# Product-key expert layer: ranking, dense products and choosing spread differently beside the gathers

## The chip, the cores and the metric

The kernel is one program on one core of a Trainium2 chip. Its engines are TensorE (PE, matrix products), VectorE (DVE), ScalarE (ACT), GpSimd (POOL, which issues the gathers) and SyncE (SP, which issues plain DMAs). The metric is the device time of the program in microseconds: 2412.99 us before the change, the median of three runs (2411.26 to 2419.2).

## What is computed

Two blocks follow each other on 512 tokens of width 1024. The first 1106 us hold everything up to the queries of the last layer and are not touched by the change. The rest is `peer`, cut here to its core:

```python
q = (xb @ w_query).reshape(TOKEN_BLOCK, P_HEADS, 2, P_HALF)
s = einsum('thpk,hpnk->thpn', q, sub_keys)
sv, si = top_k(s, P_TOPK)                    # 16 of 128 keys, twice per head
cand = sv[:, :, 0, :, None] + sv[:, :, 1, None, :]
fv, fpos = top_k(cand, P_TOPK)               # 16 of the sums per head
eidx = take_along_axis(si0 * 128 + si1, fpos)    # ids of 128 experts per token
g = softmax(fv)
act = gelu(einsum('td,thkd->thk', xb, u_tab[eidx]))
return einsum('thk,thkd->td', g * act, v_tab[eidx])
```

There are four tiles of 128 tokens. Each token picks 128 of 16384 experts (8 heads by 16), and each expert is a row of 1024 floats in `u_tab` and one in `v_tab`, in HBM.

## The kernel before

**Two ways to the products with u.** For the token tiles 0 and 1 the u rows are gathered: POOL issues one indirect DMA per expert place k (128 rows, 512 KB) and DVE takes a dot product of each row with its token (`dot`, L1972). For the tiles 2 and 3 PE computes the products with all 16384 experts: 128 dense products, each of a block of 128 experts (512 KB, loaded by SP in plain DMAs into three buffers in turn) with 256 tokens, 8 matrix instructions (`dense`, L1082). A product waits for its block; ACT copies each pair of them out of PSUM (L2502). Of these results each token needs 128, and choosing them is the work called `ext`: in each of two rounds (over the results of products 0 to 63, then of 64 to 127, which take the same place in SBUF) there are 66 steps. In a step PE spreads ids (L1109), ACT makes a one-hot matrix of them (L2513, L2515), and PE two steps later multiplies it with the results (L1095). After every fourth step DVE compares, multiplies and sums (L2010, L2015, L2019). The second round's step 33 (step 99 in all) completes tile 2: DVE adds the rounds (L2024), ACT takes the Gelu, DVE makes the weights.

**The values.** For every tile the v rows are gathered, again 128 gathers of 512 KB, and PE sums them with their weights (L1145): in each of 32 m-steps four gathers, 16 matrix instructions (the trace shows 16 weight loads and 16 products per m-step). The weights stand in a window that ACT writes (L2547). A last step on DVE (`finish`, L2034 to L2044) adds and normalises a tile.

**The stages.** POOL's gathers run in the order of `STAGES`: U0, V0, U1, V1, V2, V3, each of 128 gathers. All share 17 slots of 4 KB per partition; a gather waits until the last user of its slot is done (a dot or a value product). A gather of a U stage waits for the ids of its half (`tk_e`, L1919), and in U1 also for the dense product that the table places 8 gathers before it.

**What sets the order.** The table `BESIDE` says what lies beside the gathers of a stage. An entry `(what, a, z, first, last)` spreads pieces a to z evenly over the positions first to last: k of 0 to 127 in a U stage, m of 0 to 31 in a V stage. All engines read it, each emits its own part of a piece at that position, and each works through its instructions strictly in order. `topk` are ranking parts: 60 of them for the tiles 2, 3 and 1, 20 for each tile (eight heads' rankings, L1844 to L1860, with pair steps and decoding; the ids come with L1919 or the line behind it, the weights with ACT's L2485 behind DVE's L1955). Part 49 completes the first half of tile 1's ids, part 59 the second. `ids` is a transpose of a tile's ids on PE (L1065), which waits for them. `dense` and `ext` are counted over all stages, 128 and 132 in all. Key products on PE (L1042) go with the ranking parts.

Of the kernel before, what the change touches and what calls it, by code (L numbers as in the profile page):

```python
# [37 lines left out]
for _n, _w in ROWS:  # L38
# [15 lines left out]


BESIDE = {
    ("U", 0): [("topk", 0, 22, 10, 124), ("ids", 0, 1, 12, 12), ("ids", 1, 2, 122, 122), ("dense", 0, 64, 0, 127)],
    ("V", 0): [("topk", 22, 40, 0, 14), ("topk", 40, 50, 15, 31), ("ids", 2, 3, 17, 17), ("ext", 0, 32, 1, 15),
               ("ext", 32, 66, 18, 31)],
    ("U", 1): [("topk", 50, 60, 0, 36), ("ids", 3, 4, 44, 44), ("dense", 64, 124, 0, 127)],  # L60
    ("V", 1): [("dense", 124, 128, 0, 2), ("ext", 66, 120, 3, 31)],
    ("V", 2): [("ext", 120, 132, 0, 6)],
    ("V", 3): [],
}

# [2806 lines left out]
```

## Time and profile before

| | |
|---|---|
| median of 3 runs | 2412.99 us |
| profiled execution | 2416.05 us |
| its span | 2414.2 us |
| PE busy | 2126.6 us, 88% |
| DVE busy | 1308.9 us, 54% |
| POOL busy | 885.7 us, 37% |
| ACT busy | 643.5 us, 27% |
| data moved by DMA | 590.01 MB, mean 244 GB/s |

Busy times overlap between engines. PE's matrix products are pipelined and their ends are modelled, so its busy time isn't work at full rate. A view by stretches has one line for a stretch: start and end, length, then for each engine the busy time and the number of instructions (with PEld the weight loads), then the granted TensorE clock as a share of full speed (1.00 is 2.4 GHz, 0.5 is 1.2 GHz), the busy share of the DMA engines and GB/s. Where the view is of one source line alone, only PE and PEld stand ahead of those. A share of DMA can come out slightly over 1. A line of a view in time has the start, the duration, engine, source line, operation, tiles, shapes and count, and in brackets the idle time of that engine just before it and what ended it. A stage is bounded here by the issue of its first gather and of the next stage's first: U0 begins at 1106 us, V0 at 1370, U1 at 1591, V1 at 1824.6, V2 at 2016.6, V3 at 2211. The work of PE and DVE on a stage lies some microseconds later.

### The profile page before, as it was taken

How to read it: one execution, taken by the hardware profiler on the slowest of the kernel's cores; microseconds unless marked ns; L12 is line 12 of the kernel's file. 1: busy time of each engine (PE TensorE's matmuls, PEld its weight loads, DVE VectorE, ACT ScalarE, POOL GpSimd, SP SyncE). 2: the span in 40 equal slices, each digit the busy share in tenths (PEclk: the TensorE clock that was granted, in tenths of full speed). 3: DMA queues.
4: the chain of work that ended last, by engine and by line, in shares of the span. 5: the costliest groups of instructions: out<-in, count | busy, mean ns of one | idle time of the engine just before them, and what ended most of it. 6: DMA issues, size and time to landing. Idle time of an engine off the chain costs nothing.

```text
span 2414.2 us, 31160 instructions
## 1 busy us (share of the span) xinstructions
PE 2126.6 (88%) x12429; PEld 1576.2 (65%) x12429; DVE 1308.9 (54%) x2914; ACT 643.5 (27%) x1077; POOL 885.7 (37%) x821
## 2 busy tenths in 40 slices
PE   6999889999999997899899988899898887875775
PEld 6786879889887875887788744567786454311111
DVE  3865476776456466556988775489763233100000
ACT  3335332322354333331111133421111343200000
POOL 0410000000000000002666655556766665666664
PEclk8999999999999998999999988889999898887898
DMA  4211245444212210225999998989999999999997
GB/s 178 70 36 46 112 154 198 181 174 157 89 69 105 70 53 18 88 70 185 366 415 417 406 346 312 336 309 412 413 411 419 378 343 327 348 378 368 356 374 284
DMA packets 147056, 590.01 MB, mean 244 GB/s; under 512 B 16336, under 2 KB 16464, under 8 KB 134240
## 3 DMA queue, kind: packets, MB, share of 16 engines
q0 software_dynamic: 110592, 402.70, 43.7%
q1 hardware_dynamic: 35136, 178.80, 19.7%
q10 hardware_dynamic: 1184, 6.53, 0.7%
q8 instruction: 98, 1.61, 0.3%
q14 instruction: 46, 0.38, 0.0%
HBM read 584.29 MB, written 3.67 MB: 244 GB/s over the span
## 4 chain that ended last, share of the span: by engine, by line
PE 33%; POOL 9%; DVE 8%; issue 8%; another core or an unknown queue 6%; DMA 4%; ACT 3%; SPq 0%; POOLq 0%; DVEq 0%; ACTq 0%
PE ps L1145 7%; PE ps L1082 6%; POOL big L2655 6%; PE ps L1095 5%; PE ps L556 4%; PE ps L557 4%; PE ps L558 4%; DVE cols L1972 2%; DMA big<-vtab,big 2%; DMA raw<-ucols 2%; POOL hres L2655 1%; ACT Ir L2513 1%; PE ps L1109 1%; ACT Ir L2515 1%
## 5 line engine op out<-in xcount | busy, mean ns | idle before, releaser
L1082 PE MATMUL ps<-rowb,raw 128*128 128x256 f32 x2048 | 464.4, 387 | 24.9 <-DMA raw<-ucols 22.1
L1082 PEld LDWEIGHTS ps<-rowb,raw 128*128 128x128 f32 x2048 | 391.6, 194 | 94.4 <-issue 20.8
L1145 PE MATMUL ps<-big,cols 128*32 128x512 f32 x1380 | 365.2, 692 | 77.6 <-issue 55.1
L2655 POOL DMA_INDIRECT big<-vtab,big x345 | 332.1, 963 | 190.9 <-issue 84.0
L2578 POOL TENSOR_TENSOR small<-small,cols 128x1 f32<-128x1 f32 (+3 forms) x33 | 28.9, 876 | 896.2 <-DVE small L1590 387.8
L1145 PEld LDWEIGHTS ps<-big,cols 128*32 128x32 f32 x1380 | 73.6, 121 | 254.0 <-issue 164.2
L2655 POOL DMA_INDIRECT big<-utab,cols x144 | 178.3, 1238 | 110.3 <-issue 36.6
L1972 DVE CUSTOM_DVE_ANT_0 cols<-big 128x1024 bf16<-128x1024 f32 x144 | 173.9, 1226 | 39.5 <-DMA big<-utab,cols 29.5
L1095 PE MATMUL ps<-Aj,Ir 128*128 128x64 f32 x1024 | 161.7, 301 | 27.3 <-issue 19.7
L2015 DVE TENSOR_TENSOR cols<-cols,ps 128x512 f32<-128x512 f32 x64 | 43.9, 688 | 253.0 <-remote 124.1
L2502 ACT ACTIVATE Aj<-ps 128x512 f32<-128x512 f32 x64 | 68.1, 1067 | 418.5 <-PE ps L1082 342.4
L556 PE MATMUL ps<-xhb,whb 128*128 128x512 f32 (+1 forms) x432 | 167.2, 387 | 5.9 <-ACT fbig L2356 3.0
L1095 PEld LDWEIGHTS ps<-Aj,Ir 128*128 128x128 f32 x1024 | 144.5, 214 | 38.1 <-issue 25.6
L557 PE MATMUL ps<-xhb,wlb 128*128 128x512 f32 (+1 forms) x432 | 164.1, 380 | 0.0
L558 PE MATMUL ps<-xlb,whb 128*128 128x512 f32 (+1 forms) x432 | 163.8, 379 | 0.0
L2034 DVE TENSOR_TENSOR cols<-ps,g2b 128x512 f32<-128x512 f32 x8 | 5.2, 688 | 271.3 <-remote 139.5
L2513 ACT ACTIVATE Ir<-ps,cols 128x512 f32<-128x512 f32 x128 | 87.7, 685 | 234.0 <-remote 123.8
L556 PE MATMUL ps<-whb,ah 128*128 128x256 f32 x512 | 146.0, 285 | 1.1 <-DVE al L1624 1.1
L1145 PE MATMUL ps<-hres,cols 128*32 128x512 f32 x408 | 137.1, 738 | 10.3 <-issue 5.7
L557 PE MATMUL ps<-whb,al 128*128 128x256 f32 x512 | 143.9, 281 | 0.0
L558 PE MATMUL ps<-wlb,ah 128*128 128x256 f32 x512 | 143.8, 281 | 0.0
L2109 ACT ACTIVATE whb<-raw 128x2048 fp32r<-128x2048 f32 x51 | 97.5, 1912 | 164.3 <-DMA raw<-ff 106.8
(388 smaller groups left out, 4479.7 us busy)
## 6 DMA issues: line engine op xcount, KB each, us to landing
raw<-ucols SPq DMA_DIRECT2D x128, 512.0 KB
raw<-ff SPq DMA_DIRECT2D x32, 1024.0 KB, 4.9
raw<-w SPq DMA_DIRECT2D x24, 1024.0 KB, 4.9
raw<-ada SPq DMA_DIRECT2D x24, 1024.0 KB, 4.8
raw<-wo SPq DMA_DIRECT2D x8, 1024.0 KB, 4.9
raw<-wq SPq DMA_DIRECT2D x8, 1024.0 KB, 4.8
big<-vtab,big POOLq DMA_INDIRECT x345
hres<-x SPq DMA_DIRECT2D x8, 512.0 KB, 6.4
```

The source lines that it names most:

```text
L556: e.matmul(o, lhsT=lh, rhs=rh, start=(k == 0), stop=False)
L557: e.matmul(o, lhsT=ll, rhs=rh, start=False, stop=False)
L558: ins = e.matmul(o, lhsT=lh, rhs=rl, start=False, stop=(k == n - 1))
L1082: ins = e.matmul(PS[b][:, c:c + 256], lhsT=un[j % NU][:, k, :], rhs=h2T[k // 4][:, k % 4, :], start=(k == 0), stop=(k == 7))
L1095: ins = e.matmul(PS[b][:, c:c + JC], lhsT=Ir[:, (g % 2) * 512 + q * 128:(g % 2) * 512 + (q + 1) * 128], rhs=Atd[:, 4 * g + q, :], start=Tr ...
L1145: ins = e.matmul(PS[hf][32 * j:32 * j + 32, :], lhsT=win[:, c0:c0 + 32], rhs=gs[i][:, hf * 512:(hf + 1) * 512], start=(m == 0), stop=(m == ...
L1972: e.tensor_tensor_reduce(out=junk[k % 3], in0=gs[i], in1=h2[:, t, :], scale=1.0, scalar=0.0, op0=ALU.mult, op1=ALU.add, accum_out=act[:, t ...
L2015: e.tensor_tensor(jm[n % 2], jm[n % 2], PS[(5, 7)[n % 2]][:, :], ALU.mult).then_inc(*V.mark("ex_p", (r, n)))
L2109: e.activation(hi, raw_of(n), ACT.Copy).then_inc(*A.mark("hi", u))
L2502: e.activation(Adt[:, jl:jl + 2, :], PS[2 + pair % 2][:, :].rearrange("p (j t) -> p j t", j=2), ACT.Copy).then_inc(*A.mark("dv", pair))
L2513: e.activation(one, PS[KEYS2[g % 2]][:, :], ACT.Abs, bias=pidx).then_inc(*A.mark("ex_a", r, g))
L2655: e.indirect_dma_start(gs[i], None, utab if st == "U" else vtab, bass.IndirectOffsetOnAxis(ap=idx, axis=0)).then_inc(sems[f"l_g{i}"], 16)
```

## The change

Only the table changes. In U0 26 ranking parts in place of 22. In V0 14 parts in 13 m-steps and then 10 in 8, in place of 18 in 15 and 10 in 17; and 50 choosing steps in place of 66. U1 takes the 16 choosing steps in its first 24 positions, and has 44 dense products, from position 24 on, in place of 60 from position 0 on. V1 begins with 20 dense products in 12 m-steps in place of 4 in 3, and has 34 choosing steps in the other 20 in place of 54 in 29. V2 has 32 choosing steps in 25 m-steps in place of 12 in 7.

```diff
 BESIDE = {
-    ("U", 0): [("topk", 0, 22, 10, 124), ("ids", 0, 1, 12, 12), ("ids", 1, 2, 122, 122), ("dense", 0, 64, 0, 127)],
-    ("V", 0): [("topk", 22, 40, 0, 14), ("topk", 40, 50, 15, 31), ("ids", 2, 3, 17, 17), ("ext", 0, 32, 1, 15),
-               ("ext", 32, 66, 18, 31)],
-    ("U", 1): [("topk", 50, 60, 0, 36), ("ids", 3, 4, 44, 44), ("dense", 64, 124, 0, 127)],
-    ("V", 1): [("dense", 124, 128, 0, 2), ("ext", 66, 120, 3, 31)],
-    ("V", 2): [("ext", 120, 132, 0, 6)],
+    ("U", 0): [("topk", 0, 26, 10, 124), ("ids", 0, 1, 12, 12), ("dense", 0, 64, 0, 125), ("ids", 1, 2, 126, 126)],
+    ("V", 0): [("topk", 26, 40, 0, 12), ("topk", 40, 50, 13, 20), ("ids", 2, 3, 14, 14), ("ext", 0, 32, 1, 17),
+               ("ext", 32, 50, 18, 31)],
+    ("U", 1): [("ext", 50, 66, 0, 23), ("topk", 50, 60, 0, 36), ("ids", 3, 4, 44, 44), ("dense", 64, 108, 24, 127)],
+    ("V", 1): [("dense", 108, 128, 0, 11), ("ext", 66, 100, 12, 31)],
+    ("V", 2): [("ext", 100, 132, 0, 24)],
```

POOL's and SP's instructions stay in the same order. On PE, this is U1, the difference of the two orders; L1095 is the end of the choosing before the first dense product of U1, L1082 are dense products (8 instructions each), L1042 key products, the first L1065 the transpose of tile 1's ids, the second that of its weights at the end of the stage.

```order
 L1095 MATMUL ps<-Aj,Ir 128x64 x12
-L1082 MATMUL ps<-rowb,raw 128x256 x8
-L1042 MATMUL ps<-big 128x128 x2
-L1082 MATMUL ps<-rowb,raw 128x256 x32
-L1042 MATMUL ps<-big 128x128 x2
-L1082 MATMUL ps<-rowb,raw 128x256 x24
-L1042 MATMUL ps<-big 128x128 x2
-L1082 MATMUL ps<-rowb,raw 128x256 x96
+L1082 MATMUL ps<-rowb,raw 128x256 x64
 L1065 MATMUL ps<-cols 128x128
-L1082 MATMUL ps<-rowb,raw 128x256 x320
+L1082 MATMUL ps<-rowb,raw 128x256 x288
```

Ahead of the transpose of the ids stood 20 dense products, now 8; behind it 40, now 36. The key products of U1 now stand among the choosing steps, ahead of this piece.

On DVE, the end of V0 and the start of U1 before: two choosing events (L2010, L2015, L2019) around the last two instructions of part 49 (L1915, L1919), then the finish of tile 0 (from L2034) and the first dot (L1972).

```order
 L2010 TENSOR_TENSOR cols<-cols,big 128x512 x2
 L2015 TENSOR_TENSOR cols<-cols,ps 128x512 x2
 L2019 TENSOR_REDUCE big<-cols 128x8 x2
 L1915 SCALAR_TENSOR_TENSOR cols<-big 128x64
 L1919 CAST cols<-cols 128x64
 L2010 TENSOR_TENSOR cols<-cols,big 128x512 x2
 L2015 TENSOR_TENSOR cols<-cols,ps 128x512 x2
 L2019 TENSOR_REDUCE big<-cols 128x8 x2
 L2034 TENSOR_TENSOR cols<-ps,g2b 128x512 x2
```

After, both instructions of part 49 and the events beside them are gone from this place; the finish follows V0's last event. A few dots and one ranking later stands the first choosing event of U1:

```order
 L1972 ISA cols,big<-big 128x1024
 L1972 ISA big 128x1
 L1972 ISA cols,big<-big 128x1024
 L1972 ISA big 128x1
 L2010 TENSOR_TENSOR cols<-cols,big 128x512 x2
 L2015 TENSOR_TENSOR cols<-cols,ps 128x512 x2
 L2019 TENSOR_REDUCE big<-cols 128x8 x2
 L1972 ISA cols,big<-hres,big 128x1024
```

Part 49 now stands some 11 m-steps before the end of V0, and four choosing events stand among the first 24 dots of U1.

On PE, early V1, the difference: between the value products (L1145) stand dense products where choosing (L1109, L1095) stood.

```order
 L1145 MATMUL ps<-B2b,cols 32x512
 L1145 MATMUL ps<-big,cols 32x512
-L1109 MATMUL ps<-big,small 128x128 x4
+L1082 MATMUL ps<-rowb,raw 128x256 x8
 L1145 MATMUL ps<-big,cols 32x512 x3
 L1145 MATMUL ps<-hres,cols 32x512
 L1145 MATMUL ps<-big,cols 32x512 x3
 L1145 MATMUL ps<-hres,cols 32x512
-L1109 MATMUL ps<-big,small 128x128 x8
-L1095 MATMUL ps<-Aj,Ir 128x64 x4
+L1082 MATMUL ps<-rowb,raw 128x256 x16
 L1145 MATMUL ps<-hres,cols 32x512 x2
```

One or two dense products, 8 instructions each, stand behind each m-step's value products up to m 11.

## Rows read from the trace of the kernel before

**Rows 1.** All engines in the six stages U0, V0, U1, V1, V2, V3

```profile
core 0: us, PE busy (x) PEld busy (x) DVE busy (x) ACT busy (x) POOL busy (x), PEclk, DMA share, GB/s
1106.00:1370.00 264.00, 246.56 (x1109) 209.78 (x1109) 225.41 (x641) 33.89 (x35) 159.31 (x129) 0.97 0.94 370
1370.00:1591.00 221.00, 185.85 (x1354) 114.91 (x1357) 139.07 (x477) 89.61 (x150) 126.31 (x128) 0.86 0.89 326
1591.00:1824.60 233.60, 216.03 (x966) 181.12 (x959) 180.62 (x385) 32.40 (x33) 163.65 (x129) 0.95 1.01 405
1824.60:2016.60 192.00, 165.49 (x1135) 96.95 (x1134) 51.95 (x84) 67.85 (x115) 123.98 (x128) 0.92 0.99 374
2016.60:2211.00 194.40, 151.21 (x758) 52.60 (x762) 25.35 (x40) 26.80 (x54) 122.17 (x129) 0.83 0.94 352
2211.00:2397.00 186.00, 129.73 (x520) 29.07 (x512) 5.19 (x7) 3.25 (x15) 123.18 (x129) 0.88 0.96 367
```

**Rows 2.** The same view in two short stretches, at U1's start and in U1

```profile
...
1580.00:1600.00 20.00, 16.98 (x119) 11.58 (x119) 14.03 (x21) 7.80 (x12) 6.90 (x7) 0.79 0.45 150
...
1640.00:1660.00 20.00, 19.32 (x88) 16.17 (x87) 19.08 (x63) 2.36 (x3) 14.08 (x13) 1.00 1.03 417
...
```

**Rows 3.** Instructions of the vector engine in time, V0's end to U1's first dot

```profile
...
1587.92 1.28 DVE L2015 TENSOR_TENSOR cols<-cols,ps 128x512 f32<-128x512 f32 x2
1589.12 1.27 DVE L2019 TENSOR_REDUCE big<-cols 128x8 f32<-128x512 f32 x2
...
1590.68 0.20 DVE L1919 CAST cols<-cols 128x64 uint32<-128x64 f32 x1
...
1590.92 1.29 DVE L2010 TENSOR_TENSOR cols<-cols,big 128x512 f32<-128x512 f32 x2
1595.96 0.69 DVE L2015 TENSOR_TENSOR cols<-cols,ps 128x512 f32<-128x512 f32 x1 [3.75 <-PE ps L1095]
...
1604.69 1.23 DVE L1972 CUSTOM_DVE_ANT_0 cols<-big 128x1024 bf16<-128x1024 f32 x1
...
```

**Rows 4.** Waits from U0 to U1's end: total, times, longest

```profile
...
PE ps L1082 <- DMA raw<-ucols: 22.1, 20, 8.7
...
POOL big L2655 <- DVE cols L1919: 12.1, 1, 12.1
...
```

**Rows 5.** Scalar engine in time, in the middle of V0

```profile
...
1484.70 0.31 ACT L2485 ACTIVATE cols<-cols 128x128 f32<-128x128 f32 x1 [5.39 <-DVE cols L1955]
...
```

**Rows 6.** Value products (L1145) alone, in stretches of V0, V1, V2, V3

```profile
...
1390.00:1503.00 113.00, 45.52 (x288) 8.82 (x280) 0.83 0.91 329
1503.00:1592.50 89.50, 32.16 (x220) 6.65 (x224) 0.86 0.83 296
1840.00:1912.00 72.00, 30.50 (x192) 6.19 (x192) 0.93 1.01 406
1912.00:2034.50 122.50, 50.76 (x316) 11.61 (x320) 0.89 0.96 343
2043.50:2081.00 37.50, 14.95 (x96) 3.15 (x96) 0.77 0.89 318
2081.00:2216.50 135.50, 101.92 (x416) 21.53 (x416) 0.85 0.96 365
2233.50:2242.00 8.50, 8.34 (x64) 2.60 (x66) 0.81 0.68 246
...
```

**Rows 7.** Dense products (L1082) alone, in two stretches of U1

```profile
...
1678.00:1737.00 59.00, 58.55 (x254) 49.54 (x254) 0.95 1.02 407
1737.00:1763.00 26.00, 17.33 (x67) 14.30 (x67) 0.80 1.02 404
...
```

**Rows 8.** Vector engine in time, where U1's second half of ids is made

```profile
...
1675.43 0.20 DVE L1919 CAST cols<-cols 128x64 uint32<-128x64 f32 x1
...
```

**Rows 9.** U1's last dot and V1's first value product, in time

```profile
...
1836.02 1.23 DVE L1972 CUSTOM_DVE_ANT_0 cols<-big 128x1024 bf16<-128x1024 f32 x1 [0.79 <-DMA big<-utab,cols]
...
1840.23 1.45 PE L1145 MATMUL ps<-big,cols 128*32 128x512 f32 x4 [0.63 <-issue]
...
```

## The prediction, made before the changed kernel ran

> **What bounds the kernel now.** I read the busy shares by slice first: from 1106 us on the DMA engines stand at 8 or 9 tenths and only TensorE (PE) is nearly as busy. The question is which of the two ends last in each stage, so the second view was the busy times by stage [rows 1]. They show two kinds. In U0 and U1 both are full: DMA moves 370 and 405 GB/s, PE is busy 247 of 264 us and 216 of 234. In V0 to V3 neither is: 326 to 374 GB/s, PE 186 of 221 us down to 130 of 186. In short stretches the DMA ceiling is 417 GB/s [rows 2], so one 512 KB block, a gather or a block of weight columns, takes 524288 / 417e9 = 1.26 us of the DMA engines.
>
> Third, the vector engine (DVE) in time at the end of V0 [rows 3]. The first gather of U1 needs the ids of ranking part 49, written at 1590.68; POOL waits 12.1 us for it [rows 4], and DMA falls to 150 GB/s for 20 us [rows 2]. DVE then still finishes the last choosing of V0, whose product on PE it waits for (3.75 us at 1595.96), and its first dot of U1 starts at 1604.69 [rows 3].
>
> Fourth, how fast the value products go [rows 6]. One m-step of a V stage has 16 weight loads in that view, so the count over 16 gives the steps. With 2.4 choosing steps beside each (V0, last 14): 89.5 / 14 = 6.39 us per step. With about 1.85 (V1, last 20): 122.5 / 20 = 6.13. With 1.7 (V2, first 6): 37.5 / 6 = 6.25. With none (V2, last 26): 135.5 / 26 = 5.21. With all data in SBUF (first 4 of V3): 8.5 / 4 = 2.1. So choosing costs up to a us per step, and the last part of it is dearer than the first.
>
> Times below are in the profiled execution (span 2414.2 us, time 2416.05 us), 3 us above the median of the runs, 2412.99; I work out the difference there and add it to the median.
>
> **U0: four more ranking parts.** DVE is busy 225 of 264 us [rows 1]; 122 dots at 1.23 us [rows 3] are 150 of them, so a ranking part is (225 - 150) / 22 = 3.4 us and four are 14, inside the 39 us that DVE idles beside a full PE and DMA. I take 0; bounds 0 and +3.
>
> **V0: four ranking parts and 16 of 66 choosing steps fewer.** In m-steps 0 to 17 the ranking thins from 18 parts in 15 steps to 14 in 13. ACT, and PE behind it, waited 5.39 us there for DVE's weights [rows 5]. The 18 steps took 113 us [rows 6], 6.28 each; at V1's 6.13 they would take 110, and with part of that wait gone I take 108: -5 (bounds 0 and -10). Steps 18 to 31 carry 18 choosing steps in place of 34, 1.29 per m-step. No row has that density; the bounds are 5.21 and 6.13. I take 5.6, nearer the middle: 14 x (6.39 - 5.6) = -11 (bounds -4 and -17). V0 ends 16 us earlier. The ids of part 49 come in m-step 20, so POOL's 12.1 us wait goes. What is late next is DVE: its first dot moves only with V0's end, to 1604.7 - 16 = 1588.7.
>
> **U1, first part: DVE is the bound.** In 1640 to 1660 DVE is busy 19.08 of 20 us [rows 2]. Four choosing events come on top, each two comparisons, two products and two sums: 1.29 + 1.28 + 1.27 = 3.84 us [rows 3], 15.4 us together, ahead of the ids of the second half (part 59 at k 36). Those were written at 1675.43 [rows 8]: 1675.4 - 16 + 15.4 = 1674.8. So what V0 gives back, this takes. And PE stands behind it: the transpose of those ids (L1065, k 44) waits for DVE, and by the order of instructions 20 dense products stood ahead of it, now 8. PE, which was full here, will idle until 1675; the gathers of U1 wait for the dense count too, so they can't run ahead.
>
> **U1, second part: PE is the bound.** Behind the transpose stood 40 dense products, now 36. One takes 59 / 16 = 3.69 us (254 of 256 records shown) [rows 7]. Also 26 us for four products at 1737 [rows 7], 11 us too many: the 8.7 us wait for columns [rows 4]; it stays. So PE begins V1 at 1840.2 [rows 9] - 0.6 - 4 x 3.69 = 1824.8: 15.4 us earlier, not the 59 us that 16 products are worth. DMA has 71 gathers and 36 blocks left at k 40, 107 x 1.26 = 135 us from 1682: 1817, so it ends just ahead of PE. The chain from the last dot (1836.0) to the first value product (1840.2) [rows 9] is unchanged.
>
> **V1: 20 dense products in 12 m-steps.** These steps took 72 us with 4 dense products and the first choosing [rows 6]. Now: 20 x 3.69 = 74, and 12 value steps at the 2.1 us of [rows 6], since the gathers run a ring of 17 slots ahead: 99 us, +27. Bounds: dense work hidden fully would leave 74 (+2), the value steps at 3 us each 110 (+38). The other 20 steps have 34 choosing steps for about 37 and start with all slots landed: 122.5 less 6, bounds 0 and -17 (105 us, 5.25 each, nearly V2's pace without choosing).
>
> **V1 to V2.** The weights of V2's tokens now hang on the last choosing step of V1: a DVE sum, Gelu on ACT, a DVE product, then the windows. In the chain at V1's start the same kind of hops took 4.2 us [rows 9]; part of it lies beside the finish of V1's output. I take +2 (0 to +5). Queued behind it are PE's value products alone; POOL has 17 slots to fill.
>
> **V2: 32 choosing steps in 25 m-steps in place of 12 in 7.** Before: 37.5 + 135.5 = 173 us [rows 6]. Now 25 x 5.6 + 7 x 5.21 = 176.5: +3.5. Bounds by 5.21 and 6.13: -6 and +17. V3 is unchanged.
>
> **Sum.** -15.4 + 27 - 6 + 2 + 3.5 = +11 us: 2413 + 11 = 2424 us.
>
> **A rule against the trace.** At 1640 the DMA engines moved 417 GB/s from HBM to SBUF [rows 2]. The Trainium skill (DMA: Bandwidth & Descriptors, section Where 436 GB/s comes from) says that for such transfers the HBM side, about 358 GB/s per core, binds. By that rule the V stages, at 326 to 374 GB/s, are already full, and 16 blocks (8.4 MB) moved from U1 to V1 cost V1 what they save U1. The trace disagrees: U1 as a whole runs at 405 [rows 1].
>
> **Rivals.**
> - *The even spread hides the choosing (same).* If 1.3 choosing steps per m-step cost nothing over 5.21, V0 gains 5.5 more and V2 loses 9.5 less: 11 - 15 = -4, 2409; between this and my forecast all is within 0.3%. For: the last 0.3 to 0.5 steps per m-step seem the dear ones [rows 6]. Against: in V2 1.7 per step cost a full us.
> - *PE, no longer interrupted, catches up (faster).* The granted clock is 0.95 to 0.97 in the U stages and 0.83 to 0.92 in the V stages [rows 1]. Dense products keep it high in V1, and PE enters the last 20 m-steps with a full ring: 105 us in place of 116.5. With the rival above: -4 - 11.5 = -16, 2397. Against: once the ring is used up, POOL's issue and choosing set the pace as before.
> - *Bytes alone count (faster).* DMA totals are unchanged, so moving blocks between stages is neutral and only the 12.1 us hole of [rows 4] goes: 2401. Against: DMA idles in every V stage.
> - *Choosing stays at 6.13 per m-step (slower still).* V0 gives 7 less and V2 costs 13 more: 11 + 20 = +31, 2444.
>
> **How the numbers follow.** A measurement tells a difference from none above about 0.3%, 7 us. Forecast (2420 to 2434) 0.42; choosing hidden 0.30, all of it within 7 us; PE catches up 0.14; bytes alone 0.06; dear choosing 0.08. So faster 0.20, same 0.30, slower 0.50. The range leaves out most of the two ends: 2402 to 2440.
>
> **What would show it.** Right: U1's first gather follows V0's last at once; DVE's first dot of U1 near 1589; the ids of U1's second half near 1675 again, with PE's dense products stalled before it; V1's first value product near 1825; 12 m-steps of V1 in about 99 us; V2 within 5 us of 173. Wrong: ids well before 1665 (V0 gained over 25 us) or V1's first 12 steps under 85 us would make it faster; a pause of over 8 us at V2's start or V2 over 185 us would make it slower than forecast.

## The result, and the profile after

The changed kernel took 2429.62 us in the median of ten runs (2423.06 to 2435.09), the kernel before, run beside it, 2413.36 us (2407.68 to 2419.2). The ratio is 1.0066, with a 95% interval of 1.0048 to 1.0083: slower by 16 us. The profiled execution of the changed kernel took 2432.79 us with a span of 2431.0, so the two traces differ by 16.8 us, as the medians do.

All engines by stage, the changed kernel (the borders moved with its gathers; it answers to [rows 1], and the fences by stretches below have the same columns):

```profile
core 0: us, PE busy (x) PEld busy (x) DVE busy (x) ACT busy (x) POOL busy (x), PEclk, DMA share, GB/s
1106.00:1371.00 265.00, 249.28 (x1134) 212.79 (x1135) 232.21 (x685) 35.99 (x37) 160.69 (x128) 0.97 0.94 368
1371.00:1572.00 201.00, 168.18 (x1112) 91.92 (x1110) 116.19 (x408) 66.20 (x114) 127.75 (x129) 0.87 0.95 351
1572.00:1820.00 248.00, 201.95 (x931) 171.85 (x931) 190.95 (x401) 46.27 (x59) 157.16 (x130) 0.81 0.90 344
1820.00:2036.00 216.00, 188.32 (x1139) 117.40 (x1137) 39.69 (x66) 50.83 (x84) 125.92 (x128) 0.90 0.99 382
2036.00:2229.50 193.50, 159.31 (x998) 71.60 (x994) 43.82 (x70) 50.73 (x92) 123.08 (x130) 0.88 0.95 350
2229.50:2414.00 184.50, 131.70 (x517) 27.55 (x520) 5.19 (x7) 3.46 (x16) 123.75 (x129) 0.92 0.97 374
```

V0 is 20 us shorter by its gathers and moves more per second (351 GB/s against 326). U1 has 16 blocks less to load and is nevertheless longer: 248 us in place of 233.6, with DMA at 344 GB/s in place of 405. That line is the one to see. V1, which took the 16 blocks over, is longer by 24. In short stretches of U1's head, the view of [rows 2]:

```profile
1580.00:1600.00 20.00, 12.17 (x85) 10.27 (x81) 8.33 (x13) 6.62 (x11) 7.83 (x9) 0.65 0.70 267
1600.00:1620.00 20.00, 12.05 (x66) 11.48 (x64) 19.25 (x46) 7.76 (x12) 12.47 (x10) 0.50 0.67 216
1620.00:1640.00 20.00, 11.43 (x60) 11.16 (x61) 19.41 (x63) 5.26 (x8) 9.09 (x8) 0.50 0.67 227
1640.00:1660.00 20.00, 20.00 (x85) 17.85 (x85) 19.11 (x55) 3.71 (x5) 9.54 (x9) 0.73 0.69 230
1660.00:1680.00 20.00, 16.31 (x75) 13.70 (x73) 19.12 (x51) 1.09 (x1) 9.31 (x8) 1.00 1.02 382
...
1820.00:1840.00 20.00, 9.77 (x46) 8.14 (x44) 13.60 (x23) 3.43 (x3) 16.35 (x13) 0.88 1.03 420
```

The hole of 150 GB/s at 1580 is gone, as predicted (267 now). But where the trace of before moved 417 GB/s at 1640, 230 are moved now. DVE is full from 1600 on. Until 1640 PE is busy 11 to 12 of 20 us at a granted clock of 0.50, 1.2 GHz: it does the small products of choosing, with waits between them. The last line is U1's end: DMA moves 420 GB/s there while PE is busy only half of the time.

The vector engine in time at V0's end, which answers to [rows 3]:

```profile
1592.01 0.69 DVE L2015 TENSOR_TENSOR cols<-cols,ps 128x512 f32<-128x512 f32 x1 [11.28 <-remote]
1592.62 1.27 DVE L2019 TENSOR_REDUCE big<-cols 128x8 f32<-128x512 f32 x2
1593.99 1.29 DVE L2034 TENSOR_TENSOR cols<-ps,g2b 128x512 f32<-128x512 f32 x2
...
1598.14 1.23 DVE L1972 CUSTOM_DVE_ANT_0 cols<-big 128x1024 bf16<-128x1024 f32 x1
```

V0's last value product is at 1580.8 (1592.4 before), 11.6 us earlier. DVE then waits 11.28 us, against 3.75 in [rows 3]; by the kernel's text that wait is for PE's last choosing product, though the profile names no releaser ("remote"). So its first dot comes at 1598.1, 6.5 us earlier and not 16. The ids of the second half, which answer to [rows 8], come 8.4 us later:

```profile
1683.82 0.20 DVE L1919 CAST cols<-cols 128x64 uint32<-128x64 f32 x1
```

Dense products alone (L1082) in U1 and V1 (columns as in [rows 7]; a product has 16 records there). From 1676 to 1686 PE has nearly none: it stands before the transpose of those ids.

```profile
1646.00:1676.00 30.00, 28.30 (x120) 24.12 (x120) 0.92 0.89 316
1676.00:1686.00 10.00, 2.04 (x11) 1.46 (x9) 0.78 0.86 322
1686.00:1833.00 147.00, 132.49 (x576) 111.83 (x576) 0.95 1.01 407
1849.00:1940.00 91.00, 71.37 (x319) 59.33 (x318) 1.00 1.02 414
```

Waits of the changed kernel in U1 (total, times, longest, as in [rows 4]). The one 12.1 us wait of POOL for ids is gone, but its gathers into one of the tiles (`big`) wait 27.1 us for dots to free their slots: DVE is behind.

```profile
POOL big L2655 <- DVE big L1972: 27.1, 8, 10.0
...
DVE cols L2015 <- remote: 21.4, 2, 11.3
...
PEld ps L1082 <- DMA raw<-ucols: 13.8, 8, 9.0
```

Value products alone (L1145), which answer to [rows 6]; and V1's first one, which answers to [rows 9] (1840.23 there):

```profile
1389.00:1506.00 117.00, 49.14 (x292) 10.47 (x296) 0.84 0.94 340
1506.00:1581.00 75.00, 43.45 (x220) 8.75 (x224) 0.89 0.96 355
1843.00:1940.00 97.00, 26.71 (x192) 5.69 (x192) 0.97 1.02 415
1940.00:2052.00 112.00, 51.36 (x319) 10.83 (x320) 0.86 0.95 339
2065.00:2236.00 171.00, 100.31 (x511) 20.19 (x504) 0.89 0.95 355
```

```profile
1841.98 0.47 PE L1065 MATMUL ps<-cols,big 128*128 128x128 f32 x1 [12.21 <-DVE big L2077]
...
1843.09 1.07 PE L1145 MATMUL ps<-big,cols 128*32 128x512 f32 x2 [0.63 <-ACT cols L2547]
```

PE waited 12.2 us before the last transpose of U1. So it had ended its dense products early, and the dots, fed by DMA, came last. The same wait stood in the trace of before, shorter:

```profile
1839.28 0.33 PE L1065 MATMUL ps<-cols,big 128*128 128x128 f32 x1 [3.29 <-DVE big L2077]
```

How many gathers (L2655) POOL had issued in U1 by 1682 us, first before, then changed:

```profile
core 0: us, POOL busy (x), PEclk, DMA share, GB/s
1591.00:1682.00 91.00, 63.12 (x52) 0.93 0.99 396
```

```profile
1571.50:1682.00 110.50, 53.44 (x48) 0.67 0.77 276
```

The account between the value products (first and last weight load of each stage): V0's end 11.6 us earlier; U1, from V0's last value product to V1's first, 247.9 became 262.3 (+14.4); V1 194.2 became 208.7 (+14.5); the pause before V2 9.1 became 13.0 (+3.8); V2 -1.6; the pause before V3 17.6 became 10.8 (-6.9); V3 +4.1. The sum is +16.8.

### The profile page after: what moved, and what is told of

Read it like the earlier page. It is cut to its first block, busy times and chain, and to the rows that moved or that the text cites. A ratio compares the mean times of both kernels' runs of the same rounds, so it can differ in the third digit from the quotient of the medians.

```text
span 2431.0 us, 31147 instructions
## 1 busy us (share of the span) xinstructions
PE 2134.6 (88%) x12429; PEld 1588.7 (65%) x12429; DVE 1312.6 (54%) x2914; ACT 641.9 (26%) x1077; POOL 884.1 (36%) x821
## 4 chain that ended last, share of the span: by engine, by line
PE 37%; DVE 10%; POOL 7%; issue 7%; DMA 4%; another core or an unknown queue 4%; ACT 2%; DVEq 0%; POOLq 0%; ACTq 0%; SPq 0%
PE ps L1082 9%; PE ps L1145 8%; POOL big L2655 5%; PE ps L556 4%; PE ps L1095 4%; PE ps L558 4%; PE ps L557 4%; DVE cols L1972 3%; DMA raw<-ucols 2%; DMA big<-vtab,big 1%; POOL hres L2655 1%; PE ps L1109 1%; DMA big<-utab,cols 1%; PE ps L932 1%
## 5 line engine op out<-in xcount | busy, mean ns | idle before, releaser
L1082 PE MATMUL ps<-rowb,raw 128*128 128x256 f32 x2048 | 464.0, 387 | 21.0 <-DMA raw<-ucols 16.5
L1082 PEld LDWEIGHTS ps<-rowb,raw 128*128 128x128 f32 x2048 | 391.0, 193 | 96.2 <-issue 18.8
L1145 PE MATMUL ps<-big,cols 128*32 128x512 f32 x1380 | 359.5, 681 | 60.9 <-issue 45.2
L2655 POOL DMA_INDIRECT big<-vtab,big x345 | 333.6, 967 | 200.2 <-issue 92.1
L2015 DVE TENSOR_TENSOR cols<-cols,ps 128x512 f32<-128x512 f32 x64 | 43.5, 688 | 393.0 <-remote 266.5
L1145 PEld LDWEIGHTS ps<-big,cols 128*32 128x32 f32 x1380 | 69.7, 118 | 226.1 <-issue 155.0
L1095 PE MATMUL ps<-Aj,Ir 128*128 128x64 f32 x1024 | 170.9, 312 | 50.3 <-issue 28.3
L2655 POOL DMA_INDIRECT big<-utab,cols x144 | 169.0, 1174 | 97.9 <-issue 38.7
L1095 PEld LDWEIGHTS ps<-Aj,Ir 128*128 128x128 f32 x1024 | 154.1, 225 | 59.5 <-issue 50.9
L1972 DVE CUSTOM_DVE_ANT_0 cols<-big 128x1024 bf16<-128x1024 f32 x144 | 173.3, 1226 | 33.6 <-DMA big<-utab,cols 29.4
L1145 PE MATMUL ps<-hres,cols 128*32 128x512 f32 x408 | 137.1, 709 | 9.0 <-issue 5.9
L1190 DVE TENSOR_TENSOR wlb<-raw,whb 128x2048 fp32r<-128x2048 f32 x51 | 117.0, 2293 | 40.2 <-ACT whb L2109 37.0
```

Source lines behind the costliest of these rows:

```text
L1082: ins = e.matmul(PS[b][:, c:c + 256], lhsT=un[j % NU][:, k, :], rhs=h2T[k // 4][:, k % 4, :], start=(k == 0), stop=(k == 7))
L1095: ins = e.matmul(PS[b][:, c:c + JC], lhsT=Ir[:, (g % 2) * 512 + q * 128:(g % 2) * 512 + (q + 1) * 128], rhs=Atd[:, 4 * g + q, :], start=Tr ...
L1145: ins = e.matmul(PS[hf][32 * j:32 * j + 32, :], lhsT=win[:, c0:c0 + 32], rhs=gs[i][:, hf * 512:(hf + 1) * 512], start=(m == 0), stop=(m == ...
L1190: e.tensor_tensor(lo, raw_of(n), hi.bitcast(F32), ALU.subtract).then_inc(*V.mark("lo", u))
L1972: e.tensor_tensor_reduce(out=junk[k % 3], in0=gs[i], in1=h2[:, t, :], scale=1.0, scalar=0.0, op0=ALU.mult, op1=ALU.add, accum_out=act[:, t ...
L2655: e.indirect_dma_start(gs[i], None, utab if st == "U" else vtab, bass.IndirectOffsetOnAxis(ap=idx, axis=0)).then_inc(sems[f"l_g{i}"], 16)
```

## The experiments

Twelve runs follow, on three chips. The first four shared one, the next four another, the last four a third; each group had the kernel before beside it (2414.42, 2310.37 and 2410.64 us). The second chip is of a faster kind (last section), so the expectations of its four kernels are to be read as ratios. For all of them the measure "length of U1" is from V0's last value product to V1's first, in the one profiled execution of each; a table of it stands in the next section.

### The changed ranking, all 66 choosing steps left in V0

```diff
-    ("U", 0): [("topk", 0, 22, 10, 124), ("ids", 0, 1, 12, 12), ("ids", 1, 2, 122, 122), ("dense", 0, 64, 0, 127)],
+    ("U", 0): [("topk", 0, 26, 10, 124), ("ids", 0, 1, 12, 12), ("dense", 0, 64, 0, 125), ("ids", 1, 2, 126, 126)],
-    ("V", 0): [("topk", 22, 40, 0, 14), ("topk", 40, 50, 15, 31), ..., ("ext", 0, 32, 1, 15), ("ext", 32, 66, 18, 31)],
+    ("V", 0): [("topk", 26, 40, 0, 12), ("topk", 40, 50, 13, 20), ..., ("ext", 0, 32, 1, 17), ("ext", 32, 66, 18, 31)],
```

> The kernel before with U0 and V0 of the changed one, but all 66 first-round choosing steps left in V0 (32 in m-steps 1 to 17, 34 in 18 to 31). Theory A (the head of U1 is set by VectorE's last choosing event of V0, not by the late ids): POOL's 12.1 us hole goes, VectorE's first dot of U1 moves from 1604.7 us to about 1598 only, and the kernel gains 5 to 8 us: about 2407. Rival (the hole is the loss): the whole 12 us come back, about 2401.

2418.3 us, ratio 1.0017 (0.9996 to 1.0037). Neither expectation holds. The last 14 m-steps of V0, with the same 34 choosing steps, took 105 us (1498 to 1603) in place of 89.5, though the ranking beside them was gone but for the first three. U1's first gather followed V0's last at once, yet U1's length was 248.6 us, as with the hole (247.9). Closing the hole bought nothing in U1, and V0 became slower.

### The changed kernel with no choosing in U1

```diff
-    ("V", 0): [..., ("ext", 32, 50, 18, 31)],
-    ("U", 1): [("ext", 50, 66, 0, 23), ..., ("dense", 64, 108, 24, 127)],
+    ("V", 0): [..., ("ext", 32, 66, 18, 31)],
+    ("U", 1): [..., ("dense", 64, 108, 0, 127)],
```

> The changed kernel with its 16 choosing steps of U1 put back into V0, and the 44 dense products of U1 spread over positions 0 to 127 again. Theory A (the choosing in U1 starves the DMA engines there: VectorE is full, TensorE has no dense product for 48 us, and DMA moves 216 to 230 GB/s in place of 417, which is about 20 us of DMA work that a full DMA in the rest of U1 can't catch up): V1's first value product comes at about 1822 us in place of 1843, the kernel is about 18 us faster than the changed one: 2411. Rival (the loss is made in V1, by the 20 dense products): the changed kernel's time stays within 6 us, about 2425.

2421.98 us, ratio 1.0039 (1.0015 to 1.0064), between the two theories; its profiled execution (2416.54) was below its median. U1's length is 230.7 us: 32 less than in the changed kernel. Its V0 is again slow (99.7 us for the last 14 m-steps, 74.8 in the changed kernel), which takes 25 of the 32 back. The two windows are the first 100 us of U1 and the rest of it:

```profile
1596.60:1696.60 100.00, 76.57 (x361) 64.37 (x354) 91.25 (x240) 12.15 (x14) 63.28 (x55) 0.90 0.92 359
1696.60:1827.00 130.40, 95.29 (x399) 79.19 (x397) 97.34 (x164) 15.49 (x15) 102.50 (x85) 0.85 1.03 419
```

The head runs at 359 GB/s and the rest at 419, with PE busy only 95 of 130 us: DMA alone bounds U1's second part.

### The late half alone

```diff
-    ("U", 1): [..., ("dense", 64, 124, 0, 127)],
-    ("V", 1): [("dense", 124, 128, 0, 2), ("ext", 66, 120, 3, 31)],
-    ("V", 2): [("ext", 120, 132, 0, 6)],
+    ("U", 1): [..., ("dense", 64, 108, 0, 127)],
+    ("V", 1): [("dense", 108, 128, 0, 11), ("ext", 66, 100, 12, 31)],
+    ("V", 2): [("ext", 100, 132, 0, 24)],
```

> The kernel before with the late part of the change alone: 44 dense products in U1 (over positions 0 to 127), 20 in V1's first 12 m-steps, 34 choosing steps in V1's other 20 and 32 in V2. Theory A: U1 gets 16 blocks of DMA work shorter, 18 to 20 us; V1 gets some 15 us longer (12 m-steps 97 us for 72, the other 20 m-steps 112 for 122); V2 about the same: 2408 to 2414. Rival (V1's dense products are the loss): slower by 15 us or more, about 2430.

2413.23 us, ratio 1.0002 (0.9979 to 1.0024): theory A. Sixteen dense products fewer shorten U1 to 228.5 us, by 19: 1.2 us each, the 1.26 us of their blocks and not the 3.69 us of PE. V1's first 12 m-steps take 97 us (+25), the other 20 take 113 (-8.5). On this chip the move is neutral.

### The choosing alone, moved to U1's head

```diff
-    ("V", 0): [..., ("ext", 32, 66, 18, 31)],
-    ("U", 1): [..., ("dense", 64, 124, 0, 127)],
+    ("V", 0): [..., ("ext", 32, 50, 18, 31)],
+    ("U", 1): [("ext", 50, 66, 0, 23), ..., ("dense", 64, 124, 24, 127)],
```

> The kernel before with 16 first-round choosing steps moved from V0 into U1's positions 0 to 23, and so its 60 dense products of U1 between 24 and 127. Theory A: the dense products start about 45 us later and TensorE alone then needs 60 x 3.69 us; V0 gives back some 6 us: about 2445 to 2455. Rival (choosing steps in U1 cost only VectorE's 15.4 us, and V0 gives 10 back): about 2418.

2440.63 us, ratio 1.0104 (1.0072 to 1.0136): the direction of theory A, 4 us below its range, and far from the rival. V0 ends at 1582, but U1 is 293 us long, 45 more than with all choosing in V0. Its head and rest:

```profile
1582.00:1682.00 100.00, 77.84 (x386) 69.83 (x381) 95.64 (x244) 25.07 (x37) 57.19 (x51) 0.71 0.81 299
1682.00:1875.00 193.00, 178.26 (x802) 152.02 (x802) 113.73 (x188) 29.46 (x30) 113.33 (x93) 0.98 0.98 383
```

With 60 products to be done, most of them in this rest, PE is busy 178 of 193 us, gathers wait for it, and DMA stays at 383 GB/s: here PE is the bound. With 44, as in the changed kernel, it is not.

### The choosing pressed into 12 positions

The first round's choosing must end before dense product 64 is written over its results, so the products can start earlier only if it ends earlier.

```diff
-    ("U", 1): [("ext", 50, 66, 0, 23), ..., ("dense", 64, 108, 24, 127)],
+    ("U", 1): [("ext", 50, 66, 0, 11), ..., ("dense", 64, 108, 12, 127)],
```

> The changed kernel with U1's 16 choosing steps pressed into positions 0 to 11 (were 0 to 23) and its 44 dense products spread from position 12 on (were from 24); some 12 in place of 8 stand ahead of the transpose of the ids. Theory A (the loss is that the DMA engines starve while DVE is full at U1's head; from 1700 us they are full to the end of U1): 4 to 6 blocks are loaded earlier, at 1.26 us each, so V1 begins 5 to 8 us earlier (1843 to about 1837), time near 2423. Rival B (as predicted, PE with the products behind the transpose is the bound): 4 products fewer behind it at 3.69 us, V1 begins 15 us earlier, time near 2415. Rival C (DVE at the head alone sets the end, whatever PE and DMA do): the same work ahead of the ids, nothing moves, 2430.

Ratio 1.0078 (1.0065 to 1.0091) on the faster chip. Its time decides nothing: the changed kernel itself did not run on this chip, where the late half also costs more (below). U1's length, which for like tables agrees between the chips (246.3 to 249.3 us with 60 products and no choosing, 228.5 to 230.7 with 44), is 248.3, some 14 less than the changed kernel's 262.3 on another chip; the head ran at 309 GB/s in place of 265. About 8 of the 14 lie ahead of DVE's first dot, and the next kernel, with the same V0, shows them on this chip too. The part behind the first dot agrees better between the chips (table in the next section): 238.7 us here, 245.0 in the changed kernel. These 6 us are what theory A gives (5 to 8); rival B wanted 15, rival C none. It stays a comparison across chips.

### DVE's choosing in U1 cut to an eighth

```diff
-                iot = iotaf[:, r * JC:(r + 1) * JC]. ... .to_broadcast([128, 8, JC])
-                by8 = lambda x: x.rearrange("p (c j) -> p c j", j=JC)
+                J = 8 if 50 <= s < 66 else JC
+                iot = iotaf[:, r * JC:r * JC + J]. ... .to_broadcast([128, 8, J])
+                by8 = lambda x: x.rearrange("p (c j) -> p c j", j=JC)[:, :, 0:J]
-                    e.tensor_tensor(jm[n % 2], jm[n % 2], PS[(5, 7)[n % 2]][:, :], ALU.mult)
+                    e.tensor_tensor(by8(jm[n % 2]), by8(jm[n % 2]), by8(PS[(5, 7)[n % 2]][:, :]), ALU.mult)
```

> The changed kernel where the comparisons, products and sums of DVE's four choosing events in U1 cover 8 of each 64 numbers (so they choose only among the first 8 and leave 7/8 of that work out); every wait and all of PE's and ACT's choosing stays. It takes about 13.5 of the 15.4 us of DVE's choosing from U1's head. Theory A (DVE full at the head starves the DMA engines): ids of the second half near 1671 in place of 1684, V1's first value product near 1831 in place of 1843, time near 2418. Rival B (PE and ACT set the choosing's pace there, with the waits for PSUM and the half clock; DVE's time is cover): the ids move under 4 us, time 2427 to 2430.

Ratio 1.0047 (1.0034 to 1.0061) on the faster chip, U1's length 242.8. Without the changed kernel beside it it decides little; so it ran again on the third chip:

> The changed kernel with DVE's four choosing events in U1 over 8 of each 64 numbers (7/8 of that work left out), now with the whole change beside it on the same chip. Theory A (DVE's time at the head is what the choosing there costs): ids of U1's second half and the last dot 10 to 14 us earlier than in the changed kernel, V1's first value product too, time 10 to 14 us shorter. Rival B (PE's deferred dense products and their blocks set U1's end): the ids earlier by about 12 us, the last dot and V1 by under 5 us, time by under 5 us.

2417.18 us against the changed kernel's 2427.29 on that chip: 10 us less. U1's length is 248.7 in place of 262.7, 14 us for the 13.5 us of DVE work left out. Theory A by the time and by the length, but not by its marks in the profile: the ids came only 4 us earlier (1672.9 against 1677.0) and V1's first value product 7, because in this one profiled execution the same V0 ended 7 us later. The head and the rest of U1, first of this kernel, then of the changed kernel in the same group:

```profile
1580.60:1680.60 100.00, 76.86 (x380) 69.14 (x373) 83.89 (x244) 25.94 (x38) 58.77 (x49) 0.69 0.82 297
1680.60:1829.00 148.40, 128.54 (x560) 107.57 (x558) 107.31 (x179) 20.81 (x20) 107.91 (x85) 0.95 1.02 414
```

```profile
1573.60:1673.60 100.00, 71.02 (x360) 64.17 (x352) 85.00 (x225) 23.78 (x36) 48.06 (x43) 0.68 0.74 267
1673.60:1836.00 162.40, 133.45 (x578) 111.89 (x578) 117.53 (x199) 22.96 (x23) 121.08 (x97) 0.91 1.00 401
```

DVE's time at the head accounts for 14 of the 32 us that separate the changed kernel's U1 from one without choosing. The other 18 remain with DVE's choosing nearly gone. Some 5 of them lie ahead of DVE's first dot, in its longer wait. The rest I put down to PE's and ACT's part of the choosing and to the dense products held back behind it, whose blocks DMA can't load meanwhile (297 GB/s still, against 359); that is what is left over, and no run parts the two.

### Part 49 of the ranking earlier, nothing else

```diff
-    ("V", 0): [..., ("topk", 40, 50, 15, 31), ...],
+    ("V", 0): [..., ("topk", 40, 50, 15, 26), ...],
```

> The kernel before with one edit: ranking parts 40 to 49 in m-steps 15 to 26 of V0 in place of 15 to 31. Theory A (the hole of 12 us in POOL's issue at U1's start costs what the DMA engines lose in it): U1's first gather follows V0's last at once, DMA in 1580 to 1600 above 250 GB/s in place of 150, last dot 5 to 10 us earlier, time 2404 to 2410. Rival B (as in the kernel with all ranking of the change and all 66 choosing steps in V0: choosing without ranking between takes longer and eats the gain): V0's end 4 us later or more, time 2412 to 2419.

Ratio 1.0014 (1.0004 to 1.0024). The hole goes (POOL issues U1's first gather at 1549.9, V0's last at 1548.7) and the kernel is no faster: theory A falls. Rival B's time holds; its reason, a later end of V0, can't be read, since the kernel before has no profile on this chip. U1's length is 246.3 us, 1.6 to 3 less than with the hole on the other chips.

### That and the late half together

> The edit of part 49 and the late half of the change together (U1 with 44 dense products over all positions and no choosing, V1 and V2 as changed). If the two are independent, the time is that of the part-49 edit plus 0: 2404 to 2410 by theory A, 2412 to 2419 by rival B. A third reading: with 16 dense blocks fewer in U1 its DMA has room, so the gathers issued 12 us earlier count in full only here: 2400 to 2404.

Its edit is the two above together. Ratio 1.0049 (1.0036 to 1.0062): beside the kernel with the edit of part 49 alone, the late half costs 6.6 us on this chip, where it cost nothing on the first. Both of these expectations, "plus 0" and "counts in full only here", missed. Value products of V1's first 12 and last 20 m-steps, first with the edit of part 49 alone, then with both:

```profile
1805.00:1869.00 64.00, 33.26 (x192) 6.62 (x192) 0.98 1.03 419
1869.00:1967.00 98.00, 56.18 (x318) 11.49 (x319) 1.00 1.03 419
```

```profile
1794.00:1890.00 96.00, 25.68 (x192) 5.60 (x192) 0.98 1.03 418
1890.00:1978.00 88.00, 52.28 (x318) 11.09 (x319) 1.00 0.99 396
```

V1 was full at 419 GB/s; it takes 32 us more for its head, and gets 10 back, while U1 gives 16.4.

### The two kernels once more, on one chip

> The changed kernel once more, beside its neighbours on one chip. The chip of the last four runs took 2310 us for the kernel before, where the first took 2413 us: its V stages ran at 419 GB/s in place of 326 to 374. Theory A (choosing in U1's head starves the DMA engines, and 20 dense products in 12 m-steps of V1 hold PE at about 97 us, against 64 us there without them): slower than before on either kind of chip, 1.006 to 1.009; on the faster kind V1's steps 12 to 31 gain 10 us, not 11 to 17. Rival B (the loss depended on the slower V stages): within 0.3% of before on the faster kind.

> The kernel before once more, for its profile on this chip. Ratio 1.000 within 0.2%. If the chip is of the faster kind: V0's last 14 m-steps under 85 us (89.5 on the first chip), V1 to V3 at 415 to 420 GB/s, so that choosing costs nothing there; if of the first kind, as the profile known, 2413 us.

Changed 2427.29 us, ratio 1.0064 (1.0041 to 1.0086); before 2413.02, ratio 1.0008 (0.9988 to 1.0029). The changed kernel's ratio is inside theory A's 1.006 to 1.009. The chip was of the first kind, so what the expectations say of the faster kind was not tried. U1's length repeats, 249.3 and 262.7 us, and so do V0's last 14 m-steps, 88.0 and 74.5. U1's head and rest in the kernel before:

```profile
1599.40:1699.40 100.00, 92.84 (x423) 78.11 (x416) 88.41 (x234) 13.09 (x14) 66.80 (x57) 0.93 1.00 394
1699.40:1849.00 149.60, 133.13 (x594) 112.32 (x593) 100.95 (x168) 22.27 (x23) 111.04 (x84) 0.96 1.02 412
```

### Six choosing steps in U1 in place of sixteen

```diff
-    ("V", 0): [("topk", 22, 40, 0, 14), ("topk", 40, 50, 15, 31), ..., ("ext", 0, 32, 1, 15), ("ext", 32, 66, 18, 31)],
-    ("U", 1): [..., ("dense", 64, 124, 0, 127)],
+    ("V", 0): [("topk", 26, 40, 0, 12), ("topk", 40, 50, 13, 26), ..., ("ext", 0, 32, 1, 16), ("ext", 32, 60, 17, 31)],
+    ("U", 1): [("ext", 60, 66, 0, 7), ..., ("dense", 64, 124, 8, 127)],
```

> The kernel before with the ranking of U0 as changed, parts 40 to 49 in m-steps 13 to 26, and 6 choosing steps (60 to 65) in place of 16 moved into U1's first 8 positions; the 60 dense products spread from position 8 on; V1 and V2 as before. Theory A (the head's starvation goes with the steps moved, 26 us for 16, less than in proportion because DVE has some room at 1600): V0 ends 4 to 6 us earlier and U1 gives it all back; ratio 1.000 to 1.004. Rival B (a little choosing fits into the head for nothing): 0.997 to 0.999, a version that beats both.

2410.08 us, ratio 1.0000 (0.9982 to 1.0018): theory A's end of no change. U1's head ran at 358 GB/s and its length is 257.4 us, 8 more than before; V0 took 198 us in place of 206. What V0 gives, U1 takes. None of the versions that ran beats the kernel before.

## Why the prediction was right, and where not

The forecast was 2424 us (+11), the median is 2429.6 (+16.3), slower as said and inside the range. By steps:

- **U0: right.** V0's first value product is at 1389 against 1390.
- **V0, -16: right in size, unsure by parts.** The last 14 m-steps gave 14.5 us (11 forecast, 13.5 in the second pair). The 5 us of the first 18 can't be read: they took 113 and 118 us before, and 117, 112 and 123 in three executions of the same changed V0. So V0's end came 11.6 us earlier in the first pair, and V0 took 187 us in place of 206 in the second.
- **DVE's first dot at 1588.7: wrong, 1598.1.** The wait for PE's last choosing product took the place of the ranking that was gone. The three profiles of this V0 on chips of the first kind have the first dot 17.2 to 17.7 us behind the last value product, the two of the kernel before 12.3 and 13.7. Two more on the faster chip have 9.6, so the table alone doesn't make the longer wait.
- **U1's head, +15.4 for four choosing events, DVE-bound: shown** by cutting them to an eighth (14 us for 13.5 us of work). With the late first dot the ids came at 1683.8 and not at 1674.8.
- **The step that failed is "U1, second part: PE is the bound"** with its term of -15.4. V1's first value product came at 1843.1, not at 1824.8. I let PE decide behind the ids and let DMA end at 1817, "just ahead". The runs show DMA as the bound there in every kernel with 44 products (401 to 419 GB/s over the rest of U1; 401 holds the stretch in which PE stood before the transpose, and from 1700 us on the changed kernel moves 413 to 420), with PE 12.2 us idle before the last transpose. What counts is then the bytes that the head failed to load: 265 GB/s in its first 100 us in place of 399 are 13.4 MB, or 32 us at 417 GB/s. The 16 blocks fewer are worth 8.4 MB, 20 us. The difference, 12 us, is near the 14.4 by which U1 grew. I had seen that PE would idle and that the gathers could not run ahead, and never put a price on the idle DMA engines.

```profile
1592.40:1692.40 100.00, 94.24 (x428) 78.67 (x421) 89.76 (x236) 13.06 (x14) 68.87 (x58) 0.94 1.00 399
1692.40:1840.20 147.80, 132.10 (x588) 111.79 (x586) 99.12 (x165) 22.17 (x23) 106.05 (x83) 0.97 1.02 415
```

```profile
1580.80:1680.80 100.00, 71.16 (x360) 64.26 (x352) 85.33 (x224) 23.71 (x35) 47.44 (x43) 0.68 0.75 265
1680.80:1843.10 162.30, 133.49 (x580) 112.24 (x580) 117.48 (x200) 23.33 (x25) 123.09 (x96) 0.91 1.00 402
```

  Two things in the trace of before could have told. PE waited 3.29 us there before the same transpose, with DMA at 415 GB/s, so PE was not what ended last even with 60 products. And the 71 gathers that the prediction had left to load at 1682 us suppose POOL 17 gathers ahead of the dots: before, it had issued 52, 12 ahead. In the changed kernel it had issued 48, with 36 dots done, and SP 75 of the 108 blocks of U0 and U1. So 80 to 92 gathers and 33 to 36 blocks were left, at 1.26 us each 142 to 161 us (an estimate): DMA ends at 1824 to 1843 and not at 1817. The last dot was at 1840.0.
- **V1, 12 m-steps in 99 us: right** (97, and 97 in the late half alone). The other 20 took 111.3 us in place of 116.5. V1 to V2 +3.8 in place of +2. V2 -1.6 in place of +3.5 (+3.6 in the second pair): its first 25 m-steps took 5.7 us each, the forecast's 5.6, its last 7 took 4.2 in place of 5.2.
- **V3 unchanged: right only with the pause before it**, -6.9 and +4.1 (-7.4 and +5.6). The pause that PE no longer makes is given back in the steps behind it; no run shows why.

So U1 cost 14 us more than forecast, V0 gave 4 less, and V1 to V3 cost 13 less: the errors cancelled in part, and the near hit of the sum is luck to that extent. Of the rivals, "bytes alone" had the right rule for U1's second part and missed that the head would not be filled: its hole, 12.1 us, was the wrong one to count. Closed without the rest of the change, twice, it gave nothing. "The even spread hides the choosing" holds in V0's last 14 m-steps (75 us, 5.3 each, near the 5.21 without choosing) and not in V2 (5.7), and did not save the sum.

Where U1's time went can be read more sharply from DVE's first dot of U1, since the time before it changes from execution to execution. Both measures end at V1's first value product; us, profiled executions, chips of the second kind marked *:

| kernel | from V0's last value product | from DVE's first dot |
|---|---|---|
| before, before again | 247.9, 249.3 | 235.5, 235.6 |
| changed ranking, part 49 earlier* | 248.6, 246.3 | 235.3, 235.2 |
| late half alone, with part 49 earlier* | 228.5, 229.9 | 217.3, 218.8 |
| changed, no choosing in U1 | 230.7 | 218.6 |
| changed, changed again | 262.3, 262.7 | 245.0, 245.1 |
| choosing to an eighth, the same* | 248.7, 242.8 | 231.5, 233.2 |
| choosing in 12 positions* | 248.3 | 238.7 |
| six steps in U1 | 257.4 | 248.2 |
| choosing alone in U1 | 293.3 | 280.6 |

By the right column, 16 products fewer save 16 to 18 us, the choosing in U1's head then costs 26, and DVE's part of that is 13.6, the work left out. The other 5 of the 14.4 us by which U1 grew lie ahead of the first dot.

The rule weighed in the prediction, of the Trainium skill's DMA: Bandwidth & Descriptors, section Where 436 GB/s comes from, does not hold for this program, which runs on one core alone: on the second chip the V stages too ran at 419 GB/s. That the V stages were already full was nevertheless nearer the truth there, at that higher figure: the 16 blocks cost V1 22 us net.

## What to carry to other kernels

Where the DMA engines are full to a stage's end, price an edit by the bytes that it keeps from being loaded ahead of that end, not by the engine that looks busy: 13.4 MB not moved at the head cost more than 16 blocks fewer saved. Compare stages by their length between two fixed instructions and the GB/s of a first part and the rest, and see in a second execution how well the length repeats (the same V0 took 187 to 198 us here). A hole in a view is worth something only if what stands behind it would have gone faster; test it alone before it is counted.

## What the runs showed of the hardware

- **One program, two paces.** The kernel before took 2413, 2414 and 2411 us on three occasions and 2310 on the second group's chip. The stages V0 to V3 there, with part 49 earlier as the only edit, U1 as the second line:

```profile
1365.00:1551.00 186.00, 164.21 (x1273) 101.88 (x1274) 136.26 (x474) 81.51 (x140) 130.85 (x128) 0.90 0.97 374
1551.00:1788.00 237.00, 216.76 (x1028) 183.31 (x1026) 182.38 (x388) 37.68 (x41) 159.87 (x129) 0.96 1.00 401
1788.00:1957.00 169.00, 163.33 (x1158) 91.91 (x1157) 55.55 (x89) 68.77 (x119) 127.21 (x129) 0.99 1.03 419
1957.00:2118.00 161.00, 141.83 (x714) 42.77 (x709) 23.00 (x36) 23.62 (x49) 121.77 (x130) 0.98 1.03 419
2118.00:2280.00 162.00, 140.25 (x512) 25.20 (x512) 5.19 (x7) 3.46 (x16) 122.74 (x129) 1.00 1.03 419
```

  U1 agrees with [rows 1] (237 and 401 against 233.6 and 405). The V stages don't: 419 GB/s against 352 to 374 in V1 to V3, where [rows 1] has the DMA engines busy at 0.94 to 0.99 all the same, so the same bytes took them longer. Why is open. It changes what an edit is worth: the changed kernel's late half cost 0 on the one kind and 6.6 us on the other.
- **Choosing at half clock.** From 1600 to 1640 us, in U1's head, PE ran choosing and key products, no dense ones, was busy 11 to 12 of 20 us, and was granted 0.50; with dense products in U1's head, at 1640, [rows 2] have 1.00.
- **The same choosing, slower with less ranking beside it.** 34 choosing steps in 14 m-steps of V0 took 88 to 96.5 us with ranking spread to the end (the two profiles of before and the late half alone), and 105 and 99.7 where it ended sooner. V0 as a whole took 203 to 206 us and 218 and 212. Why is open; one execution of each was profiled.
- **A wait that the profile doesn't explain.** At the end of the changed kernel's V0 the records of PE's choosing products end at 1584 us, yet ACT, which waits for them as DVE does, goes on at 1591 and DVE at 1592, both with "remote" as the releaser. So PE's records may lie ahead of what it did there, and with them the 11.6 us of V0; by DVE's first dot V0 gave 6.5. The sum of V0 and U1 doesn't depend on this.
